# A blockwise triangular inverse on TensorE: transposed products of levels 1 and 2 moved from two array tiles to four

## The chip, the cores and the metric

One core of one Trainium2 chip. The metric is the device time of one execution in microseconds (us). The kernel before takes 3888.85 us (median of 3 runs, 3885.25 to 3891.66).

## The reference

Two transformer blocks of two layers each, on 512 tokens of width 1024, all in float32. The change touches only the first block's `rwkv7_bidir`, a linear recurrence over the tokens with 8 heads of 64, run forward and backward:

```python
def step(state, inp):
    r_t, w_t, k_t, v_t, kk_t, a_t = inp
    sa = jnp.einsum('bhij,bhj->bhi', state, -kk_t)
    state = (state * w_t[:, :, None, :] + sa[..., None] * (kk_t * a_t)[:, :, None, :]
             + v_t[..., None] * k_t[:, :, None, :])
    return state, jnp.einsum('bhij,bhj->bhi', state, r_t)
...
y = direction(0, False) + direction(1, True)
```

Everything else (pooling, differential attention, gates, feed-forward layers, the second block) is as before in both kernels.

## The kernel before, in words

The recurrence is done in chunks of 64 tokens. Within a chunk it needs the inverse of a unit triangular 64x64 matrix. There are 8 chunks, 8 heads and 2 directions: 128 such matrices in each of the two layers. They are worked on in 8 **groups** g of 16: g // 2 is the pair of heads, g % 2 the direction. A group's 16 matrices are numbered by q (0 to 3), e (which head) and p_ (which chunk of two). A half of the 128 partitions (`side(0)` or `side(1)`) holds one of two matrices.

The inverse is built by doubling. After a start X0, each **level** n (0 to 4, block sizes 2 to 32) does three products for each of the 16 matrices:

- `inv_a`: T1 = L X, which VectorE copies out of PSUM with a mask (line 1891, "the mask" below),
- `inv_x`: X' = X T1, copied out by ScalarE (line 1507),
- `inv_t`: the transpose of X', from T1 and XT, copied out by ScalarE (line 1507).

`inv_x` is left out at level 4. One product is a 64x64 by 64x64 matmul. It is float32, so it leaves two records in the trace: one step of 16 matmuls is 32 records, on PE (the matmuls) and on PEld (the weight loads). A 64x64 matmul uses one of four **array tiles**: the half of the array's rows is the half of the partitions that the operands stand on, the half of the columns is the half of the partitions of PSUM that the result goes to. A step uses all four tiles when the results of e = 1 cross to the other half, and two when none or all cross. In the kernel before the crossing is `p_ ^ e`:

| step | rows side | result side | tiles |
|---|---|---|---|
| `x0`, `r0`, `inv_a` 0, `inv_x` 0 | p_ | p_ | 2 |
| `inv_a` 1 to 4 | p_ | p_ ^ e | 4 |
| `inv_x` 1 to 3 | p_ ^ e | p_ | 4 |
| `inv_t` 0 | p_ | p_ ^ e | 4 |
| `inv_t` 1, 2, 3 | p_ ^ e | p_ ^ e | 2 |
| `inv_t` 4 | p_ ^ e | p_ | 4 |

A four-tile step writes to 256 columns of each of two neighbouring banks (`across`), a two-tile step to one bank.

**What sets the order.** Each engine runs its program in the order of one list of steps, made by `beats_of`: a group's beats are laid out one after the other, and group g + 1 starts 12 beats after group g. So while group g goes through its levels, TensorE also does the state chain of group g - 1 (`link` 1 to 7, some 8 matmuls each, whose state ScalarE copies), and VectorE and ScalarE do the preparation of group g + 1:

- `prep_w` on VectorE, after the mask of level 1: lines 1834 and 1835, and then 1837 where g + 1 is even, but 1840 and 1841 where g + 1 is odd (one instruction more),
- `prep_a`: four Exp on ScalarE, which wait for `prep_w`'s end, between the copies of level 1 and those of level 2; lines 1845 to 1850 on VectorE after the mask of level 2,
- `prep_b`, `prep_ar` on VectorE after the mask of level 3 (lines 1858 to 1868), which `gram` of g + 1 on TensorE waits for.

TensorE's order in one level is `inv_a` n, `link`, `inv_x` n, `inv_t` n, `link`, `inv_a` n + 1. `inv_a` n + 1 waits for ScalarE's copy of `inv_x` n; `inv_x` n waits for the mask of level n and the copy of `inv_t` n - 1. Each copy waits its turn behind what ScalarE has before it. `prep` of the last group's successor does not exist, so group 7 has no such neighbour, and group 0 has no `link` beside it. After group 7 the layer goes on with weights whose ring memory the recurrence had borrowed (`ring_back`).

## Time and profile before

| what | value |
|---|---|
| runs | 3885.25, 3891.66, 3888.85 us |
| the profiled execution | 3887.13 us, its span 3885.3 us |
| mean granted TensorE clock | 0.991 of full |
| PE busy | 3717.4 us (96%) |
| DVE, ACT, POOL busy | 43%, 37%, 36% |
| line 1891, the mask, in the first layer's recurrence | 32 x 0.69 us |

How to read it: PE is TensorE's matmuls, PEld its weight loads, DVE VectorE, ACT ScalarE, POOL GpSimd. The two recurrences lie at 98 to 375 us and 1216 to 1490 us of the span. Line 1134 is the helper that issues every matmul of the first block that is not a weight product, and line 1507 the one that issues every ScalarE instruction there, so a step is told by its place, its operands and its count: `inv_a` reads `arena,ring`, `inv_x` and `inv_t` read `arena` alone and follow each other in one row (x64). Group and level are written as (g, n).

### The profile page before, as it was taken

Reading aid. Unit: us, or ns where it says so; the run is one execution under the profiler, and the core shown is the slowest. Engines: PE = TensorE matmul, PEld = TensorE weight load, DVE = VectorE, ACT = ScalarE, POOL = GpSimd, SP = SyncE. Lnnn points to the kernel's source line nnn. Section 1 sums busy time; section 2 is a strip of 40 time slices with the busy share of each in tenths; the row PEclk is TensorE's granted clock in tenths of the full one; section 3 lists DMA queues with packets and bytes.
Section 4 is the critical chain, followed back from the end, with each engine's and each line's share of the span. In section 5 each row is a group of like instructions: output and inputs, shape, how many; then the busy total and the mean of one; then the engine's idle time right before and its main releaser. Section 6 shows DMA issues by size and latency. Waiting matters only on the chain.

```text
span 3885.3 us, 67218 instructions
## 1 busy us (share of the span) xinstructions
PE 3717.4 (96%) x28976; PEld 2990.7 (77%) x28976; DVE 1684.8 (43%) x2722; ACT 1448.4 (37%) x2468; POOL 1382.3 (36%) x581
## 2 busy tenths in 40 slices
PE   8888999999999898999999999999999999999999
PEld 7777768888887786687888876578888776688887
DVE  6554541477135554612683158515111377332112
ACT  3454252323324443522223243634222436433222
POOL 5001324444443002144444444234444353234443
PEclk9999999999999999999999999999999999999999
DMA  3001212266221001122473222112222221122222
GB/s 146 3 4 46 84 64 100 87 245 238 87 87 44 4 4 67 70 111 87 160 266 148 87 93 82 44 66 103 102 94 87 107 89 50 60 87 87 87 108 87
DMA packets 37151, 356.66 MB, mean 92 GB/s; under 512 B 4224, under 2 KB 4352, under 8 KB 17920
## 3 DMA queue, kind: packets, MB, share of 16 engines
q1 hardware_dynamic: 19584, 278.93, 19.4%
q10 hardware_dynamic: 17280, 73.48, 5.4%
q8 instruction: 232, 3.80, 0.4%
q14 instruction: 55, 0.45, 0.0%
HBM read 350.29 MB, written 2.10 MB: 91 GB/s over the span
## 4 chain that ended last, share of the span: by engine, by line
PE 84%; DVE 7%; ACT 4%; issue 2%; DMA 1%; PEld 1%; POOL 0%; PEldq 0%; DVEq 0%; SPq 0%; ACTq 0%; POOLq 0%
PE banks L768 23%; PE banks L770 23%; PE banks L769 23%; PE banks L1134 10%; PE banks L2200 3%; ACT arena L2356 2%; ACT arena L1507 2%; DMA ring<-stream 1%; PE banks L2282 1%; DVE arena L1996 1%; PE banks L1261 1%; DVE arena L1891 1%; DVE x L2757 0%; PE banks L1459 0%; DVE arena L2007 0%
## 5 line engine op out<-in xcount | busy, mean ns | idle before, releaser
L866 POOL TENSOR_TENSOR ring_r<-ring,hi_ring 128x1024 fp32r<-128x1024 f32 x490 | 1200.8, 2455 | 2174.0 <-ACT hi_ring L857 2173.4
L768 PE MATMUL banks<-xT_r,ring_r 128*128 128x512 f32 (+1 forms) x2480 | 949.0, 383 | 10.8 <-issue 6.8
L770 PE MATMUL banks<-xT_r,hi_ring 128*128 128x512 f32 x2096 | 826.5, 394 | 0.0
L769 PE MATMUL banks<-x_lo_r,hi_ring 128*128 128x512 f32 x2096 | 823.6, 393 | 0.0
L857 ACT ACTIVATE hi_ring<-ring 128x1024 fp32r<-128x1024 f32 x490 | 511.2, 1046 | 724.1 <-DMA ring<-stream 293.5
L768 PEld LDWEIGHTS banks<-xT_r,ring_r 128*128 128x128 f32 x2480 | 470.6, 190 | 105.2 <-issue 11.9
L770 PEld LDWEIGHTS banks<-xT_r,hi_ring 128*128 128x128 f32 x2096 | 394.5, 188 | 93.1
L769 PEld LDWEIGHTS banks<-x_lo_r,hi_ring 128*128 128x128 f32 x2096 | 396.3, 189 | 88.0 <-issue 1.4
L1134 PE MATMUL banks<-arena 64*64 64x64 f32 (+4 forms) x7456 | 342.4, 249 | 52.0 <-DVE arena L1891 22.8
L1507 ACT ACTIVATE arena<-banks 128x512 f32<-128x512 f32 x366 | 214.6, 596 | 388.6 <-PE banks L770 231.4
L770 PE MATMUL banks<-hi_ring,pairs 128*128 128x512 f32 x864 | 342.3, 396 | 0.0
L769 PE MATMUL banks<-ring_r,pairs 128*128 128x512 f32 x864 | 342.0, 396 | 0.0
L768 PE MATMUL banks<-hi_ring,pairs 128*128 128x512 f32 x864 | 340.6, 394 | 0.0
L1134 PEld LDWEIGHTS banks<-arena 64*64 64x64 f32 (+2 forms) x7456 | 262.4, 139 | 96.1 <-DVE arena L1891 27.8
L871 DVE TENSOR_TENSOR pairs<-arena,pairs 128x512 fp32r<-128x512 f32 x108 | 82.6, 765 | 430.8 <-ACT pairs L862 430.6
L2356 ACT ACTIVATE arena<-banks 128x512 f32<-128x512 f32 (+3 forms) x288 | 141.6, 504 | 306.2 <-PE banks L770 219.1
L1507 ACT ACTIVATE arena<-banks,small 128x512 f32<-128x512 f32 (+2 forms) x254 | 119.5, 482 | 255.8 <-PE banks L770 160.6
L769 PEld LDWEIGHTS banks<-ring_r,pairs 128*128 128x128 f32 x864 | 162.3, 188 | 39.7
L768 PEld LDWEIGHTS banks<-hi_ring,pairs 128*128 128x128 f32 x864 | 162.4, 188 | 39.3 <-POOL ring_r L866 0.8
L770 PEld LDWEIGHTS banks<-hi_ring,pairs 128*128 128x128 f32 x864 | 163.1, 189 | 37.0
L862 ACT ACTIVATE pairs<-arena 128x512 fp32r<-128x512 f32 x108 | 68.1, 631 | 311.9 <-PE banks L770 307.1
L769 PE MATMUL banks<-ring_r,xT_r 128*128 128x512 f32 (+1 forms) x448 | 169.9, 379 | 0.0
(274 smaller groups left out, 5400.3 us busy)
## 6 DMA issues: line engine op xcount, KB each, us to landing
ring<-stream SPq DMA_DIRECT2D x132, 2048.0 KB, 7.7
arena<-ada ACTq DMA_DIRECT2D x96, 512.0 KB, 4.9
arena<-ln_rows ACTq DMA_DIRECT2D x5, 1024.0 KB, 7.6
arena<-edge ACTq DMA_DIRECT2D x4, 1024.0 KB, 5.1
arena<-edge ACTq DMA_DIRECT2D x2, 1792.0 KB, 8.1
arena<-pack ACTq DMA_DIRECT2D x2, 1485.0 KB, 6.7
arena<-pack ACTq DMA_DIRECT2D x2, 1200.5 KB, 5.8
x<-x_in SPq DMA_DIRECT2D x4, 512.0 KB, 7.5
```

Of the source, the lines that this page charges most:

```text
L768: first = nc.tensor.matmul(out_, left[1], right[0], start=start, stop=False)
L769: low = nc.tensor.matmul(out_, left[0], right[1], start=False, stop=False)
L770: return first, low, nc.tensor.matmul(out_, left[0], right[0], start=False, stop=stop)
L857: nc.scalar.activation(feed.hi(n), feed.raw(n), ACT.Copy).then_inc(split_hi, 1)
L862: nc.scalar.activation(feed.hid_pair(n)[0], feed.hid[:, n, :], ACT.Copy).then_inc(hid_hi, 1)
L866: nc.gpsimd.tensor_tensor(feed.raw(n, ring_r), feed.raw(n), feed.hi(n).bitcast(F32), ALU.subtract).then_inc(split_lo, 1)
L871: nc.vector.tensor_tensor(lo, feed.hid[:, n, :], hi.bitcast(F32), ALU.subtract).then_inc(hid_lo, 1)
L1134: return nc.tensor.matmul(out_, lhsT, rhs, start=start, stop=stop)
L1261: ins = nc.tensor.transpose(bank[b][:, q * P:(q + 1) * P], src, C("ident"))
L1507: return nc.scalar.activation(out_, in_, func, **kw)
L2200: return nc.tensor.matmul(out_, lhsT, rhs, start=start, stop=stop)
L2356: return nc.scalar.activation(out_, in_, func, **kw)
```

## The change

The side that holds T1 and XT now depends on the level. `turned_side` gives it: p_ at levels 0 and 5, e at level 2, p_ ^ e at levels 1, 3 and 4. T1 of level n stands on the side of level n, and XT moves from the side of level n to the side of level n + 1 through `inv_t` n. So `inv_t` 1 goes from p_ ^ e to e and `inv_t` 2 from e to p_ ^ e: four tiles each. `inv_t` 3 stays at p_ ^ e, with two.

Four-tile products go to two banks. Bank 6 has no free neighbour, so `inv_t` 1 and 2 are written to the banks of the other direction (`2 - b0` and the next), which group g + 1 uses for `prep` before and for `gram` after. `inv_t` 1 therefore waits for `prep` of g + 1 to be copied out of both.

In all four-tile steps, those that had four tiles before too, the bank is now chosen by the array's rows side (it was e), and the four matmuls of one q are issued in the order of (result side, rows side): before, e was the outer loop and p_ the inner one. The copies follow the new places; `wu` reads XT at `p_ ^ e` instead of e. The number of matmuls and copies is the same.

```diff
-        banks_a, banks_x, banks_t = (b0,), (b0,) if n else (6,), (b0,) if n == 0 or last else (6,)
+        banks_a, banks_x, banks_t = (b0,), (b0,) if n else (6,), ((b0,), (2 - b0,), (2 - b0,), (6,), (b0,))[n]
...
-        return name == "inv_t" and level in (0, len(LEVELS) - 1) or name in ("inv_a", "inv_x") and level > 0
+        return name == "inv_t" and level != len(LEVELS) - 2 or name in ("inv_a", "inv_x") and level > 0
+
+    def turned_side(level, p_, e):
+
+        return p_ if level in (0, len(LEVELS)) else e if level == 2 else p_ ^ e
...
+                    if (name, args[1]) == ("inv_t", 1) and g < GROUPS - 1:
+                        drained(pe, uses, "prep", g + 1, only=1)
...
+                def turned_at(p_, e):
+                    return side(turned_side(level, p_, e)), turned_side(level - 1, p_, e) if 0 < level < len(LEVELS) - 1 else e
+
+                def tiles_of_array(p_, e):
+                    f = turned_side(level, p_, e)
+                    return (f, p_) if name == "inv_a" else (p_, f) if name == "inv_x" else (turned_side(level + 1, p_, e), f)
+
                 for q in range(4):
...
+                    for p_, e in sorted(HALVES, key=lambda pair: tiles_of_array(*pair)) if wide(name, level) else ():
+                        to, r = tiles_of_array(p_, e)
+                        h, i = turned_at(p_, e)
...
+                        ins = mm(across(banks[0])[side(to), r, q * CH:(q + 1) * CH], left, right, True, True)
...
-                            ins = mm(bank[banks[q // 2]][h, (q % 2 * 2 + e) * P:(q % 2 * 2 + e + 1) * P], XT[d][h, 2 * q + e, :],
+                            ins = mm(bank[banks[q // 2]][h, (q % 2 * 2 + e) * P:(q % 2 * 2 + e + 1) * P], XT[d][h, 2 * q + (p_ ^ e), :],
```

On TensorE, the first layer's group 1 at level 2: `inv_x` (rows 617 and 618), then `inv_t` (rows 619 and 620). Before:

```order
611 L1134 MATMUL banks<-arena 64x64 [waits halves_done,bank5_free]
612 L1134 MATMUL banks<-arena 64x64
613 L1134 MATMUL banks<-arena,ring 64x64 [waits bank5_free]
614 L1134 MATMUL banks<-arena,ring 64x64
615 L1134 MATMUL banks<-ring 64x64 x2
616 L1134 MATMUL banks<-arena 64x64 x2
617 L1134 MATMUL banks<-arena 64x64 [waits bank6_free,bank2_free]
618 L1134 MATMUL banks<-arena 64x64 x15
619 L1134 MATMUL banks<-arena 64x64 [waits bank6_free,bank2_free]
620 L1134 MATMUL banks<-arena 64x64 x15
```

(rows 611 to 616 are a `link` of group 0). The same place after:

```order
611 L1138 MATMUL banks<-arena 64x64 [waits halves_done,bank5_free]
612 L1138 MATMUL banks<-arena 64x64
613 L1138 MATMUL banks<-arena,ring 64x64 [waits bank5_free]
614 L1138 MATMUL banks<-arena,ring 64x64
615 L1138 MATMUL banks<-ring 64x64 x2
616 L1138 MATMUL banks<-arena 64x64 x2
617 L1138 MATMUL banks<-arena 64x64 [waits bank0_free,bank2_free]
618 L1138 MATMUL banks<-arena 64x64 x15
619 L1138 MATMUL banks<-arena 64x64 [waits bank0_free,bank2_free]
620 L1138 MATMUL banks<-arena 64x64 x15
```

Nothing moves: the steps stand in the same places, and the wait for bank 6 became one for bank 0.

On ScalarE, the copies of `inv_x` and `inv_t` of the same group at level 1 (rows 160, 161) and level 2 (rows 167, 168), as they stand after the change:

```order
160 L1525 ACTIVATE arena<-banks 128x2x4x64 [waits bank2_full]
161 L1525 ACTIVATE arena<-banks 128x2x4x64 [waits bank0_full]
162 L1525 ACTIVATE arena<-banks,small 128x64 [waits bank5_full]
163 L1525 ACTIVATE small<-arena 128x8 [waits prep_sum]
164 L1525 ACTIVATE arena<-arena 128x512 x2
165 L1525 ACTIVATE arena<-arena 128x512 [waits act_step]
166 L1525 ACTIVATE arena<-banks,small 128x64 [waits bank4_full]
167 L1525 ACTIVATE arena<-banks 128x2x4x64 [waits bank2_full]
168 L1525 ACTIVATE arena<-banks 128x2x4x64 [waits bank0_full]
```

Before, rows 161 and 168 were `arena<-banks 128x512 [waits bank6_full]`; the other rows and the order are the same. Rows 163 to 165 are `prep_a` of group 2: they stand ahead of the state copy (166) and of the copies of level 2.

## Rows read from the trace of the kernel before

**Rows 1.** The page, the chain that ended last, share of the span by line.

```profile
PE banks L768 23%; PE banks L770 23%; PE banks L769 23%; PE banks L1134 10%; PE banks L2200 3%; ACT arena L2356 2%; ACT arena L1507 2%; DMA ring<-stream 1%; PE banks L2282 1%; DVE arena L1996 1%; PE banks L1261 1%; DVE arena L1891 1%; DVE x L2757 0%; PE banks L1459 0%; DVE arena L2007 0%
```

**Rows 2.** Busy time by window, first recurrence: length, busy by engine (records), clock, DMA.

```profile
98.00:375.00 277.00, 241.53 (x6760) 209.50 (x6758) 139.09 (x215) 126.05 (x255) 0.93 (x1) 0.97 0.05 16
```

**Rows 3.** Timeline, weight loads, group 4: start, length, operation, count, [idle <-releaser].

```profile
247.11 1.07 PEld L1134 LDWEIGHTS banks<-arena,ring 64*64 64x64 f32 x30
...
253.49 1.51 PEld L1134 LDWEIGHTS banks<-arena 64*64 64x64 f32 x64 [0.52 <-DVE arena L1891]
...
255.33 0.60 PEld L1134 LDWEIGHTS banks<-arena,ring 64*64 64x64 f32 x30
...
257.14 1.96 PEld L1134 LDWEIGHTS banks<-arena 64*64 64x64 f32 x67 [0.56 <-DVE arena L1891]
```

**Rows 4.** Timeline, VectorE, group 4.

```profile
255.78 0.69 DVE L1841 TENSOR_TENSOR arena<-arena 128x512 f32<-128x512 f32 x1
256.39 0.68 DVE L1891 TENSOR_TENSOR arena<-banks,const 128x512 f32<-128x512 f32 x1
...
260.26 0.69 DVE L1891 TENSOR_TENSOR arena<-banks,const 128x512 f32<-128x512 f32 x1 [0.81 <-PE banks L1134]
```

**Rows 5.** Timeline, ScalarE, group 4.

```profile
256.62 1.79 ACT L1507 ACTIVATE arena<-arena 128x512 f32<-128x512 f32 x3
258.33 0.30 ACT L1507 ACTIVATE arena<-banks,small 128x64 f32<-128x64 f32 x1
258.52 1.07 ACT L1507 ACTIVATE arena<-banks 128x512 f32<-128x512 f32 x2
```

**Rows 6.** Timeline, weight loads, group 3.

```profile
226.07 0.60 PEld L1134 LDWEIGHTS banks<-arena,ring 64*64 64x64 f32 x32
...
229.67 0.60 PEld L1134 LDWEIGHTS banks<-arena,ring 64*64 64x64 f32 x32
...
233.71 1.08 PEld L1134 LDWEIGHTS banks<-arena 64*64 64x64 f32 x36 [0.45 <-DVE arena L1868]
```

**Rows 7.** Timeline, VectorE, group 3.

```profile
223.50 0.69 DVE L1891 TENSOR_TENSOR arena<-banks,const 128x512 f32<-128x512 f32 x1 [3.68 <-PE banks L1134]
...
225.82 0.69 DVE L1837 TENSOR_TENSOR arena<-arena 128x512 f32<-128x512 f32 x1
226.89 0.69 DVE L1891 TENSOR_TENSOR arena<-banks,const 128x512 f32<-128x512 f32 x1 [0.38 <-PE banks L1134]
```

**Rows 8.** Timeline, ScalarE, group 3.

```profile
225.05 0.60 ACT L1507 ACTIVATE arena<-banks 128x512 f32<-128x512 f32 x1 [1.15 <-PE banks L1134]
...
228.69 0.60 ACT L1507 ACTIVATE arena<-banks 128x512 f32<-128x512 f32 x1
```

**Rows 9.** Chain of waits, second layer, group 5: start, length, what.

```profile
1399.79 0.70 DVE arena L1891
...
1403.97 2.58 PE banks L1134 x108
```

**Rows 10.** Timeline, weight loads, group 7.

```profile
341.08 0.37 PEld L1134 LDWEIGHTS banks<-arena,ring 64*64 64x64 f32 x14
342.03 0.36 PEld L1134 LDWEIGHTS banks<-arena,ring 64*64 64x64 f32 x17 [0.58 <-issue]
```

**Rows 11.** Timeline, ScalarE, group 7.

```profile
340.06 0.60 ACT L1507 ACTIVATE arena<-banks 128x512 f32<-128x512 f32 x1 [1.15 <-PE banks L1134]
```

**Rows 12.** Busy time by window, first layer, group 0, around its level 2.

```profile
137.00:144.00 7.00, 5.71 (x151) 5.36 (x147) 5.10 (x9) 4.01 (x8) 0.00 (x0) 0.53 0.01 2
```

**Rows 13.** Timeline, ScalarE, group 0.

```profile
141.09 0.60 ACT L1507 ACTIVATE arena<-banks 128x512 f32<-128x512 f32 x1 [0.21 <-PE banks L1134]
```

**Rows 14.** Timeline, weight loads, group 0.

```profile
142.31 0.18 PEld L1134 LDWEIGHTS banks<-arena,ring 64*64 64x64 f32 x1
```

**Rows 15.** Timeline, weight loads: gram of group 3, then wu of group 2.

```profile
204.25 1.08 PEld L1134 LDWEIGHTS banks<-arena 64*64 64x64 f32 x36 [0.88 <-DVE arena L1868]
...
210.63 1.75 PEld L1134 LDWEIGHTS banks<-arena 64*64 64x64 f32 x32 [0.40 <-ACT arena L1507]
```

More of the change, by code:

```diff
@@ L1281, in step @@
                 level = args[1] if len(args) > 1 else 0
-                for q in range(4):
-                    for e in range(2):
-                        for p_ in range(2):
-                            n, straight, crossed = 2 * q + e, side(p_), side(p_ ^ e)
-                            h = crossed if level and name in ("inv_x", "inv_t") else straight
-                            to = crossed if name == "inv_a" and level or name == "inv_t" and level < len(LEVELS) - 1 else straight
-                            left, right = {"x0": (XT[d][h, n, :], C("ident2")[h]), "r0": (GM[d][h, q, e, 1, 0, :], V[g // 2 % 2][h, q, e, :]),
-                                           "inv_a": (GM[d][h, q, e, 0, 0, :], X[d][h, n, :]), "inv_x": (XT[d][h, n, :], T1[d][h, n, :]),
-                                           "inv_t": (T1[d][h, n, :], XT[d][h, n, :])}[name]
-                            at = (4 * e + q if wide(name, level) else n) * CH
-                            to = across(banks[0])[to, at:at + CH] if wide(name, level) else bank[banks[0]][to, at:at + CH]
-                            ins = mm(to, left, right, True, True)
+                def turned_at(p_, e):
+                    return side(turned_side(level, p_, e)), turned_side(level - 1, p_, e) if 0 < level < len(LEVELS) - 1 else e
@@ new lines, in tiles_of_array @@
+                def tiles_of_array(p_, e):
+                    f = turned_side(level, p_, e)
+                    return (f, p_) if name == "inv_a" else (p_, f) if name == "inv_x" else (turned_side(level + 1, p_, e), f)
+                for q in range(4):
+                    for p_, e in sorted(HALVES, key=lambda pair: tiles_of_array(*pair)) if wide(name, level) else ():
+                        to, r = tiles_of_array(p_, e)
+                        h, i = turned_at(p_, e)
+                        if name == "inv_a":
+                            i = turned_side(level - 1, p_, e) if level > 1 else e
+                            left, right = GM[d][side(p_), q, e, 0, 0, :], X[d][side(p_), 2 * q + i, :]
+                        else:
+                            left, right = XT[d][h, 2 * q + i, :], T1[d][h, 2 * q + (p_ if level else e), :]
+                            left, right = (left, right) if name == "inv_x" else (right, left)
+                        ins = mm(across(banks[0])[side(to), r, q * CH:(q + 1) * CH], left, right, True, True)
+                    for e, p_ in () if wide(name, level) else HALVES:
+                        h, n = turned_at(p_, e)[0] if name == "inv_t" else side(p_), 2 * q + e
+                        left, right = {"x0": (XT[d][h, n, :], C("ident2")[h]), "r0": (GM[d][h, q, e, 1, 0, :], V[g // 2 % 2][h, q, e, :]),
+                                       "inv_a": (GM[d][h, q, e, 0, 0, :], X[d][h, n, :]), "inv_x": (XT[d][h, n, :], T1[d][h, n, :]),
+                                       "inv_t": (T1[d][h, 2 * q + p_, :], XT[d][h, 2 * q + turned_at(p_, e)[1], :])}[name]
+                        ins = mm(bank[banks[0]][h, n * CH:(n + 1) * CH], left, right, True, True)
@@ L1581, in step @@
                 filled(b, n)
-                f((XT if name == "inv_t" else X)[args[0] % 2].rearrange("p (q e) t -> p e q t", e=2),
-                  across(b).rearrange("p (e q t) -> p e q t", e=2, q=4), ACT.Copy).then_inc(bank_free[b], 1)
+                f((XT if name == "inv_t" else X)[args[0] % 2].rearrange("p (q r) t -> p r q t", r=2),
+                  across(b).rearrange("p r (q t) -> p r q t", q=4), ACT.Copy).then_inc(bank_free[b], 1)
             elif name in ("x0", "inv_x", "inv_t"):
@@ L1890, in step @@
                 if wide(name, lev):
[L1891 to L1892 removed]
+                    V.tensor_tensor(T1[g % 2].rearrange("p (q r) t -> p r q t", r=2),
+                                    across(b).rearrange("p r (q t) -> p r q t", q=4),
+                                    masks.rearrange("p (r q) t -> p r q t", r=2), ALU.mult).then_inc(bank_free[b], 1)
                 else:
```

4 lines of the change are left out of this document (1 added, 3 removed).

## The prediction

> **What bounds the kernel now.** I read the chain by line first: three quarters of the span are the weight products of lines 768 to 770 and their kind, and line 1134, which holds the recurrence's small products, has 10% [rows 1]. So the change can only act inside the two recurrences. The window of the first shows PE busy for 241.5 of 277 us, VectorE for 139 and ScalarE for 126 [rows 2]; the second is nearly the same length (1216 to 1490 us). A busy share of 87% does not say that TensorE is the bound in each beat, because VectorE and ScalarE stand in the same loop. So I went to the timelines, engine by engine, and asked at each level what `inv_a` and `inv_x` wait for.
>
> **What the change takes off TensorE.** A two-tile step and a four-tile step of the same kind stand in one view: 30 loads of `inv_a` (4, 0) on two tiles take 1.07 us, 30 loads of `inv_a` (4, 2) on four take 0.60 us [rows 3]. The difference, 0.47 us, is what `inv_t` gives up at one level. The row of 1.51 us with 64 loads is `inv_x` (four tiles) and `inv_t` (two) one behind the other; it should become some 1.05 us. There are 2 levels x 8 groups x 2 layers = 32 such steps: 32 x 0.47 = 15.0 us of TensorE's time. That is the most that the change can bring, if each beat ended with TensorE.
>
> The Trainium skill speaks against this much (TensorE: Matmul & The Clock Gate, "Wait — 56ns, not 53.3ns?"): from one matmul's start to the next it never sees less than about 25 ns. By that a step of 32 records could not go under 0.80 us, and a new four-tile step would save some 0.15 us instead of 0.47 (an estimate from that page); every gain below would be a third, some 1.3 us in all. The 30 loads in 0.60 us [rows 3] are 20 ns apart at most, so this trace does not obey that floor and I give it no chance.
>
> **Even groups (2, 4, 6 in both layers, 0 in the second: seven).** Nothing, and this is the step that most of the forecast hangs on.
> Level 1: `inv_t` (4, 1) would end 0.47 earlier, and so could `link` and `inv_a` (4, 2), up to the point where the copy of `inv_x` is done. But the mask of level 2 starts at 256.39 with no idle time ahead of it, directly behind line 1841 of `prep_w` [rows 4]. VectorE's own queue from the mask of level 1 on sets that moment, however early `inv_a` (4, 2) comes. `inv_x` (4, 2) starts at 257.14 as before.
> Level 2: ScalarE does the Exps of `prep_a` from 256.62 to 258.41, then the state copy, and then the copy of `inv_x` at 258.52 with that of `inv_t` directly behind it [rows 5]. `inv_x` had been finished before (it is the first third of the row from 257.14 [rows 3]). `inv_a` (4, 3) waits for that copy, not for `inv_t`. The Exps wait for line 1841, which the change does not reach. So the mask of level 3 at 260.26, though it shows "0.81 <-PE" [rows 4], is late through ScalarE's queue, and `gram` of group 5 behind it keeps its time.
>
> **Odd groups with a successor (1, 3, 5 in both layers: six).** Here `prep_w` is one instruction shorter. In group 3 it ends at 226.51, and the mask of level 2 waits for PE until 226.89 [rows 7]. The copy of `inv_x` (3, 1) ends at 225.65 [rows 8], so `inv_a` (3, 2) can start some 0.06 later, at 225.71, instead of 226.07 [rows 6]: 0.36 earlier, and the mask too. At level 2 the copy of `inv_x` again stands behind the Exps and ends at 229.29 [rows 8], whatever TensorE does: `inv_a` (3, 3) starts at 229.35 instead of 229.67 [rows 6], and mask, `prep_b` and `gram` at 233.71 follow it. So group 3 gains 0.32, not 0.94. From the mask of level 1 (223.50) to that earliest start are 5.85 us. I hold it against a group without a disturbance, group 5 of the second layer: its mask of level 1 is at 1399.79 and `inv_a` (5, 3) ends at 1403.97 + 2.58 = 1406.55 [rows 9]. With 5.85 and the 0.74 that `inv_a` lasts it could end at 1406.38: 0.17. I take 0.25 for each of the six, between the two: 1.5 us.
>
> **Group 7 (twice).** No preparation runs beside it. The copy of `inv_x` (7, 1) ends at 340.66 [rows 11], `inv_a` (7, 2) started at 341.08 [rows 10] and can start at 340.72: 0.36. Level 2 has the same pattern. 2 levels x 2 layers x 0.36 = 1.4 us, all on the path, since the rest of the layer waits for group 7.
>
> **Group 0 of the first layer.** Here the mean granted clock is 0.53 [rows 12], so nearly all of this stretch runs at the lower level, 1.2 GHz, and a two-tile step is longer. The copy of `inv_x` (0, 2) ends at 141.69 [rows 13], so `inv_a` (0, 3) can start at 141.75 instead of 142.31 [rows 14]: 0.56. Level 1 can add between nothing and 0.47; I take 0.3. Together 0.9 us.
>
> **What costs.** One wait is added, in 14 places: `inv_t` 1 waits until `prep` of the next group has been copied out. Behind it in TensorE's queue stand a `link` and `inv_a`. `prep` is some 4 us older than `inv_t` 1 and its copies stand ahead of those of level 0, which `inv_a` 1 has already waited for, so I count nothing. `gram` of the next group now needs the banks of `inv_t` 2, whose copy `inv_x` 3 has waited for: nothing. ScalarE's copies of `inv_t` read two banks instead of one; the copies of `inv_x` do that now in the same 0.60 us [rows 8].
> The order and the banks of all other four-tile steps change too (7 steps of `inv_a` and `inv_x` and 2 of `inv_t` in each group, 144 in all). Their new pattern is that of `gram`: bank by rows side, (result, rows) in order. `gram` with four tiles and 128 columns takes 1.08 us for 36 loads (32 and a `link`'s 4), `wu` on two tiles and 128 columns 1.75 for 32 [rows 15]. So that pattern runs on four tiles. For 64 columns it is not in the trace: the bounds are no change and the two-tile rate, 0.47 more per step. I take no change.
>
> **The sum.** 1.5 + 1.4 + 0.9 = 3.8 us off the profiled execution: 3887.1 - 3.8 = 3883.3 us. That execution was 1.7 us under the median of the three runs, so for a median I say **3885.0 us**. A measurement of this kernel can tell about 0.2%, 7.8 us, from no change; its three runs alone spread over 6.4 us. My forecast is below that.
>
> **The rivals.**
> *TensorE was the bound after all* (12%). If what looks like cover moves along (the Exps of `prep_a` and the masks shift with the copies), the full 15.0 us come off: 3874. For it speaks PE's busy share in the window [rows 2]; against it, VectorE without idle time ahead of the mask [rows 4]. With half of it, 7.5 us, the time is 3881.
> *Instructions come too late* (9%, slower). TensorE stands still now and then in the middle of a step for want of instructions: 0.58 us inside `inv_a` (7, 2), put down to "issue" [rows 10]. Place: `inv_x`, `inv_t`, `link`, `inv_a` of levels 1 and 2, which now all run at the four-tile rate, 1.9 us in a row instead of 2.3. Price: some 0.6 to 0.8 us per new stop. If each of the 16 groups had one more on its path, 16 x 0.7 = 11.2 less the 3.8 gained is 7.4 slower: 3896. It decides from about 5 new stops for a gain lost, from 17 for a measurable loss. Against it: the same instructions are fetched, and in even groups a stop falls into the slack that the change widens. The Trainium skill (Runtime: NRT & Kernel Launch, "Instruction fetch mechanics") has instructions fetched in blocks ahead and calls this hidden by a slow issue; by it this rival would cost nothing. The row with 0.58 disagrees.
> *The new order halves the old four-tile steps* (4%, slower). Two matmuls with the same result side follow each other now. If they no longer ran side by side, 112 steps of `inv_a` and `inv_x` would cost 0.47 more, 53 us; with half of it covered 26, less 3.8: 3911. Rows 15 speak against it.
> *The change does nothing at all* to the time, since covers are wider than I read (15%): 3887 to 3889.
>
> **Chances.** My forecast has 60%, its own range 3881 to 3888. Faster by over 0.2%: the first rival and the edge of the forecast, 17%. Slower by over 0.2%: half of the second rival and the third with a share for a clock that falls in more places, 11%. Within 0.2%: 72%. The range 3877 to 3892 leaves out most of the first rival and the slow ends.
>
> **What would show it.** In the profile after: the x64 row of `inv_x` and `inv_t` at levels 1 and 2 near 1.05 us; the mask of level 2 in even groups still directly behind line 1841, and `inv_a` 3 still behind ScalarE's copy; in odd groups and group 7 `inv_a` 2 starting 0.06 us after the copy of `inv_x`; from the mask of level 1 to `gram` of the next group unchanged in even groups and 0.2 to 0.3 shorter in odd ones; line 1134's "issue" time as before. I am wrong if even groups become shorter, if `inv_a` alone takes over 0.7 us for its 32 loads, or if more than a handful of new "issue" stops stand in the levels.

## The result and the profile after: slower by 0.17%

| | median | runs | ratio to before, 95% |
|---|---|---|---|
| before | 3891.66 us | 19, 3883.51 to 3897.32 | 1 |
| changed | 3897.67 us | 19, 3892.70 to 3903.81 | 1.0017 [1.0011, 1.0023] |

0.17% of 3890 is 6.6 us slower; 3.8 us faster had been forecast. The profiled execution took 3895.01 us with a span of 3893.2, against 3887.13 and 3885.3. In these two executions the mean granted clock is the same 0.991. Over many executions it is not: the 19 of the changed kernel have 0.9891 on average, and the 114 of the kernel before that were timed beside the experiments have 0.9908 to 0.9911 in their four series. (The 19 of before in the table above have no clock on record.) What that is worth stands below, under "The clock as a rival".

What the change was to do to the array, it did. The view by windows has, in the columns of [rows 2], both recurrences of the changed kernel:

```profile
98.00:375.00 277.00, 234.34 (x6745) 201.06 (x6743) 137.92 (x212) 122.73 (x251) 0.00 (x0) 0.97 0.03 10
1216.00:1490.00 274.00, 234.09 (x6741) 200.88 (x6740) 137.42 (x212) 122.21 (x250) 2.41 (x1) 0.98 0.02 5
```

PE is busy for 7.2 us less than in [rows 2] in the first recurrence (and for 5.0 us less in the second, 239.06 before). It is idle longer, and the view of waits (engine, line, waited for: us in total, times, longest) says what the weight loads of the recurrence waited for. Before, first and second recurrence:

```profile
PEld banks L1134 <- issue: 18.6, 41, 1.3
...
PEld banks L1134 <- issue: 17.9, 41, 1.3
```

The changed kernel (its line 1138 is line 1134 of before, 1525 is 1507, 1909 is 1891):

```profile
PEld banks L1138 <- issue: 26.1, 50, 2.1
...
PEld banks L1138 <- issue: 24.1, 51, 1.6
```

"issue" is time in which TensorE waited for no engine and no transfer that the profile shows. It is 36.5 us before and 50.2 after (the two rows added), and a part of it is on the path. The chain of waits by line, first and second recurrence, before:

```profile
by line: PE banks L1134 58.1%; ACT arena L1507 10.2%; issue 6.1%; DVE arena L1891 3.7%; PE banks L1261 3.7%; PE banks L768 2.2%; PE banks L770 2.0%; PE banks L769 2.0%; DVE arena L1858 1.7%; DVE arena L1868 1.5%; DVE arena L1859 1.5%; DVE a
...
by line: PE banks L1134 55.7%; ACT arena L1507 11.1%; issue 5.3%; PE banks L1261 3.7%; DVE arena L1891 3.5%; PE banks L768 2.3%; PE banks L770 2.2%; PE banks L769 2.2%; DVE arena L1835 1.8%; DVE arena L1858 1.7%; DVE arena L1868 1.6%; DVE a
```

and changed:

```profile
by line: PE banks L1138 52.4%; ACT arena L1525 12.2%; issue 7.8%; PE banks L1265 3.6%; DVE arena L1909 3.0%; DMA ring<-stream 2.8%; PE banks L768 2.2%; PE banks L770 2.0%; PE banks L769 2.0%; DVE arena L1853 1.8%; DVE arena L1876 1.2%; DVE 
...
by line: PE banks L1138 52.9%; ACT arena L1525 11.7%; issue 7.0%; PE banks L1265 3.4%; DVE arena L1909 3.3%; PE banks L768 2.6%; PE banks L770 2.5%; PE banks L769 2.4%; DVE arena L1853 1.8%; DVE arena L1876 1.7%; DVE arena L1886 1.6%; DVE a
```

The share of "issue" rises by 1.7% of the window in both: 1.7% x (277 + 274) = 9.4 us more on the path. This is a sign and no sum, since other shares move by as much: PE's line falls by 5.7% and 2.8%, ScalarE's rises by 2.0% and 0.6%, and a transfer of 2.8% stands in the first chain of the changed kernel.

**Where the time goes.** The masks are the same instructions in both kernels, four in each group, so the time from one to the next can be compared place by place. From the first group's mask of level 1 to group 7's last, the first recurrence takes 216.90 us before (135.19 to 352.09) and 219.62 changed (136.01 to 355.64), the second 213.79 (1254.57 to 1468.37) and 217.67 (1256.37 to 1474.04). That is 6.6 us more, of the 7.9 us between the two profiled spans. All 62 intervals, changed less before, in us:

| groups | mask 1 to 2 | mask 2 to 3 | mask 3 to 4 | to the next group's first |
|---|---|---|---|---|
| group 0 of the first layer | -0.3 | -0.7 | +0.7 | 0.0 |
| odd, with a successor (six) | -1.5 | +3.4 | 0.0 | +1.0 |
| even (seven) | +0.2 | +3.5 | +0.1 | -0.2 |
| group 7 (twice) | -0.5 | +0.7 | +0.1 | |

So there is a gain from level 1 to level 2, in the odd groups and in group 7, and it is more than lost from level 2 to level 3, in even groups as well. The largest single losses are group 2's in both layers, 1.5 us each. VectorE's masks of levels 1, 2 and 3 there, first layer, before and changed, and the weight load of the changed kernel that makes the third one late:

```profile
193.73 0.69 DVE L1891 TENSOR_TENSOR arena<-banks,const 128x512 f32<-128x512 f32 x1 [3.68 <-PE banks L1134]
197.38 0.68 DVE L1891 TENSOR_TENSOR arena<-banks,const 128x512 f32<-128x512 f32 x1
201.11 0.69 DVE L1891 TENSOR_TENSOR arena<-banks,const 128x512 f32<-128x512 f32 x1 [0.67 <-PE banks L1134]
```
```profile
195.00 0.69 DVE L1909 TENSOR_TENSOR arena<-banks,const 128x512 f32<-128x512 f32 x1 [3.68 <-PE banks L1138]
198.65 0.68 DVE L1909 TENSOR_TENSOR arena<-banks,const 128x512 f32<-128x512 f32 x1
203.88 0.69 DVE L1909 TENSOR_TENSOR arena<-banks,const 128x512 f32<-128x512 f32 x1 [2.17 <-PE banks L1138]
```
```profile
203.21 0.37 PEld L1138 LDWEIGHTS banks<-arena,ring 64*64 64x64 f32 x18 [1.38 <-issue]
```

The last row is the second part of `inv_a` (2, 3): TensorE stood for 1.38 us in the middle of the step.

**Where a stop lies.** Group 7 of the first layer, weight loads, changed kernel (it answers to [rows 10]):

```profile
342.87 1.12 PEld L1138 LDWEIGHTS banks<-arena 64*64 64x64 f32 x67 [0.50 <-DVE arena L1909]
...
344.37 0.30 PEld L1138 LDWEIGHTS banks<-arena,ring 64*64 64x64 f32 x11
345.09 0.37 PEld L1138 LDWEIGHTS banks<-arena,ring 64*64 64x64 f32 x19 [0.42 <-issue]
...
347.97 0.24 PEld L1138 LDWEIGHTS banks<-arena,ring 64*64 64x64 f32 x8
350.34 0.44 PEld L1138 LDWEIGHTS banks<-arena,ring 64*64 64x64 f32 x24 [2.14 <-issue]
...
355.24 1.25 PEld L1138 LDWEIGHTS banks<-arena,ring 64*64 64x64 f32 x38 [1.43 <-issue]
```

`inv_a` (7, 2) stops for 0.42 us, `inv_a` (7, 3) for 2.14, each in the middle of a step. From stop to stop, here and behind the stop of group 2 above, the windows show (length, PE, PEld, DVE, ACT, POOL, clock, DMA share, GB/s):

```profile
345.09:350.34 5.25, 2.88 (x126) 2.60 (x125) 0.69 (x1) 1.60 (x4) 0.00 (x0) 1.00 0.01 3
203.21:208.35 5.14, 3.62 (x126) 3.24 (x126) 3.26 (x6) 1.51 (x3) 0.00 (x0) 1.00 0.02 3
```

Some 126 matmuls, as many loads and a few semaphore instructions: 256 TensorE instructions. Counted through the whole trace, every stop of over 0.3 us inside a step lies at the same remainder of the instruction's number by 256. The page names the carrier:

```profile
q8 instruction: 232, 3.80, 0.4%
```

232 packets of 16384 bytes (3.80 MB) for TensorE's 59540 instructions: 256 in a packet, 64 bytes each. A packet takes 0.9 to 1.5 us. Of the changed kernel's 101 blocks in the two recurrences, 30 begin with such a stop, and in 29 of these the first instruction comes 1.2 to 1.6 us after the packet's end. So these stops are waits for a block of instructions. I call the place where one block ends and the next begins a **border**. Stops of over 0.3 us at borders: 13 with 10.2 us before, 30 with 26.1 us in the changed kernel.

That also shows why the recurrence is sensitive. A level is three steps of 64 instructions (32 loads, 32 matmuls), two `link`s of 32 and 5 semaphore instructions: 261, about one block. It lasts 3.60 us in group 3 of the kernel before (`inv_a` at 226.07 and 229.67 [rows 6]).

### The profile page after: what moved, and what is told of

It reads as the page before. It is cut to its first block, busy times and chain, and to the rows that moved or that the text cites. A ratio compares the mean times of both kernels' runs of the same rounds, so it can differ in the third digit from the quotient of the medians.

```text
span 3893.2 us, 67232 instructions
## 1 busy us (share of the span) xinstructions
PE 3709.0 (95%) x28976; PEld 2978.1 (76%) x28976; DVE 1695.7 (44%) x2722; ACT 1446.9 (37%) x2468; POOL 1384.3 (36%) x581
## 4 chain that ended last, share of the span: by engine, by line
PE 82%; DVE 8%; ACT 4%; issue 3%; DMA 1%; POOL 1%; PEld 1%; PEldq 0%; DVEq 0%; ACTq 0%; SPq 0%; POOLq 0%
PE banks L768 23%; PE banks L770 22%; PE banks L769 22%; PE banks L1138 9%; PE banks L2219 3%; ACT arena L1525 2%; ACT arena L2375 2%; PE banks L2301 1%; DMA ring<-stream 1%; DVE arena L2015 1%; DVE arena L2701 1%; PE banks L1265 0%; DVE arena L2700 0%; DVE x L2776 0%; DVE arena L1909 0%
## 5 line engine op out<-in xcount | busy, mean ns | idle before, releaser
L1138 PE MATMUL banks<-arena 64*64 64x64 f32 (+4 forms) x7456 | 333.3, 251 | 58.8 <-DVE arena L1909 25.8
L1138 PEld LDWEIGHTS banks<-arena 64*64 64x64 f32 (+2 forms) x7456 | 252.0, 140 | 101.9 <-issue 31.5
L768 PEld LDWEIGHTS banks<-hi_ring,pairs 128*128 128x128 f32 x864 | 162.4, 188 | 39.4 <-POOL ring_r L866 0.8
```

Source lines behind the costliest of these rows:

```text
L768: first = nc.tensor.matmul(out_, left[1], right[0], start=start, stop=False)
L1138: return nc.tensor.matmul(out_, lhsT, rhs, start=start, stop=stop)
```

## The experiments

In all of them "time" is a median, with its ratio to the kernel before, timed beside it, and the 95% interval. The medians of before in these series go from 3888.68 to 3891.66 us, so the ratios are to be compared and not the times. "Issue" is the sum of the two rows of the view of waits (36.5 us before, 50.2 changed). "Stops" are those of over 0.3 us at borders.

**1. The order and the banks alone, and one level alone.** The order and the banks of all other four-tile steps as in the changed kernel, but `inv_t` 1 and 2 on two tiles in bank 6, and without the added wait for `prep`:

```diff
-        banks_t = ((b0,), (2 - b0,), (2 - b0,), (6,), (b0,))[n]
+        banks_t = ((b0,), (6,), (6,), (6,), (b0,))[n]
-        return name == "inv_t" and level != len(LEVELS) - 2 or ...
+        return name == "inv_t" and level in (0, len(LEVELS) - 1) or ...
-        return p_ if level in (0, len(LEVELS)) else e if level == 2 else p_ ^ e
+        return p_ if level in (0, len(LEVELS)) else p_ ^ e
...
-                    if (name, args[1]) == ("inv_t", 1) and g < GROUPS - 1:
+                    if (name, args[1]) == ("inv_t", -1) and g < GROUPS - 1:
```

> The changed kernel with the side of T1 and XT at p_ ^ e on all levels 1 to 4, so inv_t 1 and 2 have two array tiles and bank 6 again. Kept of the change: in all four-tile steps the bank is chosen by rows side and the four matmuls of a q are issued in the new order. Theory A (instructions come too late: with four tiles in inv_t 1 and 2 the levels use up a block of 256 TensorE instructions faster than the next one arrives, 29 stops for want of instructions in both recurrences instead of 13): the time is that of before, within 2 us, with about 13 stops of together some 10 us. Theory B (the new order or banks cost time in the old four-tile steps): all of the loss is here, some 6 to 7 us above before. Theory C (the waits for the other direction's banks): as before.

Then four tiles at level 1 only (`level in (0, 1, ...)`, banks `(2 - b0,)` there), and at level 2 only; the wait for `prep` stands at the `inv_t` that has four tiles. In these two, two products of a two-tile `inv_t` go to the same place, so a part of XT is lost; the instructions and their tiles are those named.

> Four tiles in inv_t at level 1 alone; level 2 keeps two tiles and bank 6. Theory A: stops lie between 13 and 29 and the time between before and the changed kernel, 0 to 6 us above before; not simply half, since where a block ends is a matter of place. Theory B: the full 6 to 7 us. Theory C (the wait of inv_t 1 for prep of the next group, which is here): the full loss here, none with level 2 alone.

> Four tiles in inv_t at level 2 alone; level 1 keeps two tiles and bank 6. Theory A: as with level 1 alone, 0 to 6 us above before and 13 to 29 stops. Theory B: the full 6 to 7 us. Theory C: no loss, since level 2 comes 4 us after the wait for prep's copies matters.

| run | time | ratio | issue | stops |
|---|---|---|---|---|
| order and banks alone | 3888.57 us | 0.9995 [0.9986, 1.0004] | 32.7 us | 12, 8.6 us |
| level 1 alone | 3893.86 us | 1.0013 [1.0004, 1.0022] | 44.2 us | 27, 20.6 us |
| level 2 alone | 3892.64 us | 0.9998 [0.9989, 1.0007] | 38.9 us | 19, 13.7 us |

The order and the banks cost nothing that an interval of 0.1% (3.5 us) can tell, and the 26 to 53 us of the prediction's rival are ruled out. The loss comes back with four tiles at level 1. With level 2 alone there is none, though "issue" and stops grow there too. Taken by themselves, these two rows are also what the theory of the added wait had forecast, the full loss at level 1 and none at level 2; experiment 3 has to decide on that. The recurrences' own lengths, taken from mask to mask as above, are 427.8 us for the order alone, 434.8 for level 1, 428.6 for level 2, with 430.7 before and 437.3 changed.

**2. How fast can TensorE get instructions?** The kernel before, with 256 extra products on four tiles (512 weight loads and 512 matmuls, four blocks) and then 256 on two, before the first `gram`, without a wait between them (the wait for the two banks is moved ahead of them):

```diff
+                if (layer, g, n) == (0, 0, 0):
+                    c0 = CONST["gram0"][0]
+                    for tiles in (4, 2):
+                        for turn in range(64 if tiles == 4 else 64):
+                            for to, r in sorted(HALVES) if tiles == 4 else ((0, 0), (1, 1), (0, 0), (1, 1)):
+                                mm(bank[banks[r]][side(to), turn % 8 * CH:(turn % 8 + 1) * CH], const[side(r), c0:c0 + CH],
+                                   const[side(r), c0 + CH:c0 + 2 * CH], True, True)
```

> The kernel before, and ahead of the first gram of the first layer 256 products of 64x64 by 64x64 of constants on four tiles, in the changed order and banks, and then 256 on two tiles; no wait inside, results overwritten by gram. Each half is 1024 TensorE instructions (512 weight loads, 512 matmuls), four blocks of 256. By the array alone the first half takes 512 x 14.4 ns = 7.4 us and the second 512 x 29 ns = 14.8 us. Theory A: the supply sets both; stops every 256 instructions, 3.5 to 5.2 us from one to the next, 14 to 20 us for each half. If the supply were not a bound (rivals B, C): 7.4 and 14.8 us and no stops. B would show in a first half without stops but longer than 7.4 us.

It took 3917.68 us in its one execution. Timeline of the weight loads (start, length, operation, count, idle before):

```profile
124.61 1.96 PEld L1134 LDWEIGHTS banks<-const 64*64 64x64 f32 x128 [1.08 <-issue]
128.06 1.95 PEld L1134 LDWEIGHTS banks<-const 64*64 64x64 f32 x128 [1.50 <-issue]
131.52 2.82 PEld L1134 LDWEIGHTS banks<-const 64*64 64x64 f32 x128 [1.50 <-issue]
135.52 3.81 PEld L1134 LDWEIGHTS banks<-const 64*64 64x64 f32 x128 [1.18 <-issue]
139.52 3.81 PEld L1134 LDWEIGHTS banks<-const 64*64 64x64 f32 x128 [0.20 <-issue]
```

This is the clearest measurement of the study. The array does 128 loads and their matmuls on four tiles in 1.96 us, but the next 128 begin 3.45 us after the first: 1.50 us of standing still at each of the two borders behind a block that is all on four tiles. The row of 131.52 holds the change from four tiles to two: 2.82 us, then 1.18 us of standing still. On two tiles alone the same number takes 3.81 us and the stop is 0.20. Four tiles are worth 1.85 us of array time per block, of which 0.55 arrive (4.00 to 3.45 us). At 3.45 us a block an instruction costs 13.5 ns, though the array does one in 7.7 ns here (1.96 us for 256). The first half as a whole was a miss: it took 11.9 us (120.65 to 132.52), where 14 to 20 were expected; at its start TensorE still had part of a block at hand, and the borders behind it lie 3.45 us apart, the low end of the 3.5 to 5.2 expected. The second half took 16.9 us.

**3. The added wait alone.** As the first run of experiment 1, but with the changed kernel's wait for `prep` (14 places):

```diff
-                    if (name, args[1]) == ("inv_t", -1) and g < GROUPS - 1:
+                    if (name, args[1]) == ("inv_t", 1) and g < GROUPS - 1:
```

> The changed kernel with the transposed products of levels 1 and 2 on two tiles and in bank 6, as in the run of the order alone, but with the changed kernel's wait for the next group's preparation at inv_t of level 1 (14 places). Theory C (that wait or what it orders costs the time): 3894 to 3898 us, as the changed kernel. Theory A: no instruction comes faster than before and few are added, so stops of 9 to 11 us in sum and the time within 1.5 us of the run of the order alone: a ratio of 0.9990 to 1.0004 against before.

3891.91 us, 1.0001 [0.9992, 1.0010]; issue 39.0 us, stops 20 with 14.2 us, where 9 to 11 us of stops were expected. The ratio is in the range of the supply theory, the median 3.3 us above the run without the wait where 1.5 were allowed. The 14 waits are 14 instructions more, so the borders drift too, and the two can't be told apart here. Without four tiles in `inv_t` 1 and 2 the wait brings no loss to the kernel before that its interval (0.1%) can tell, which answers the question that experiment 1 left. Not tested is the wait together with four tiles, so that what it costs there is open.

**4. Moving the borders.** Waits on a semaphore long set, put where TensorE waits anyway; two of them are one instruction, each 0.106 us. They are to change nothing behind them but where the borders fall. In the kernels with 16, 32 and 64 instructions they stand ahead of the first `gram`:

```diff
                 A, B = ARI[g % 3], BB[g % 2]
+                for _ in range(K if (layer, g) == (0, 0) else 0):
+                    pe.wait_ge(const_loaded, 16)
                 if n == 0:
```

The loop runs once for each half of the first `gram`, so it adds 2 K waits, which are K instructions (K = 16, 32 or 64). The first three expectations leave open whether waits or instructions count; the traces show 32 and 64 instructions. The added waits are not quite free: TensorE stands for 1.9 and 1.8 us at this place with 16 or 32 instructions more, for 1.9 and 3.1 with 64, so that the last cost 1.3 us. All of this is put down to "issue" and is contained in that column below, 3.6 us (4.9 at 64) in both kernels alike, but not in the rows 0 and "64, elsewhere".

> The same with half as many extra waits (32 ahead of each of the two parts), so that the blocks' borders lie a quarter of a block or less from those of the changed kernel. Theory A: stops of over 0.3 us again at the same remainder by 256 and at a third set of steps; number 25 to 35, sum 22 to 34 us; time 3894 to 3904 us. Theories B and C: stops at the steps of the changed kernel, time within 1 us of it.

> The changed kernel with 64 more waits on the constants' semaphore in TensorE's stream ahead of the first gram of group 0 and 64 ahead of its second part (a semaphore that has long been set, so that they wait for nothing), packed two to an instruction: if they all stand ahead of the recurrence, every later TensorE instruction is 64 or 128 places further on in the stream; TensorE is waiting for the preparation there anyway. Theory A (a block of 256 TensorE instructions comes too late; the stops lie where the stream passes from one block to the next): all stops of over 0.3 us in the recurrences still lie at the same remainder of the instruction's number by 256, so at other steps of the program than in the changed kernel: the stops of 1.5 us within inv_a of group 2, level 3 and of 2.3 us within inv_a of group 7, level 3 are gone from there. Their number stays near 30 and their sum within 22 to 34 us (26 in the changed kernel), the time within 3 us below to 6 us above the changed kernel's: 3894 to 3904 us. Theory C (a bank or the earlier wait for the next group's preparation) and theory B (the order of the products): the stops stay at the same steps, since the steps, banks and waits are the same, and the time within 1 us.

> The kernel before with the same extra waits as in the run with half as many. Theory A: the 13 stops of the kernel before lie at other steps; their sum 8 to 15 us (10 before), the time within 2 us below to 4 us above the kernel before: a ratio of 0.9995 to 1.001. Theories B and C: stops at the same steps and the same time.

Then the same 64 instructions in the kernel before, and 16 in both:

> The kernel before with the same extra waits as the changed kernel has in its run with 64 more instructions (the profiles of the last runs show how far these waits shift the stream: two waits are one instruction, so 32 and 64 instructions, an eighth and a quarter of a block, not 64 and 128). They cost 1.3 us at the first gram, as there. Theory A: stops of 8 to 15 us in sum, at other steps than in the kernel before; with the 1.3 us a time of 3889 to 3894 us. If the change's worth hangs on where the blocks' borders fall, the changed kernel at this place (3891.2 us) stands 3 us below to 3 us above this one, not 6.6 us above as without a shift. If the loss of the changed kernel had nothing to do with the borders, this run would be at 3884 to 3886 us.

> The changed kernel with 16 more instructions ahead of the recurrence, in TensorE's waits for the first group's preparation (8 in each). Theory A: stops of over 0.3 us 20 to 30, 16 to 26 us in sum, at the same remainder by 256; a time between those at a shift of 0 and of 32 instructions: 3890 to 3898 us. Without a part of the borders in it: 3897 to 3898 us, as the changed kernel.

> The kernel before with the same 16 instructions. Theory A: 8 to 15 us of stops, 3889 to 3892 us; the changed kernel at this shift is 0 to 7 us above it.

Last 96 in both, 64 of them in TensorE's first waits for the input, and 64 in the changed kernel all at that place:

```diff
                     pe.wait_ge(ident_loaded, 16)
+                for _ in range(64 if (layer, which) == (0, 2) and tt < 2 else 0):
+                    pe.wait_ge(ident_loaded, 16)
```

> The changed kernel with 96 more instructions ahead of the recurrence, as empty waits: 64 of them (32 and 32) in TensorE's first two waits for the input, some 12 and 4 us long, and 32 in its waits for the first group's preparation. They should cost nothing by themselves. The supply of instructions: 20 to 30 stops of 18 to 27 us, at steps again other than before; 3888 to 3898 us. If the loss depends on where the borders fall, this kernel stands 2 us below to 8 us above the kernel before at the same shift; if the runs at 0 and 16 were above it for another reason than the borders, it would stand 6 to 8 us above.

> The kernel before with the same 96 instructions. The supply of instructions: 8 to 14 us of stops, 3887 to 3892 us.

> The changed kernel at the shift of 64 instructions once more, but with the extra instructions in the waits for the input, so that the 1.3 us at the first gram should be saved. If the position of the borders sets the stops: stops over 1 us at the steps that had them in the other run with 64 (inv_x of group 1 at level 2, links of group 2, layer 1's inv_a of group 3 at level 3 and links of group 5), a sum of 19 to 26 us and 3889 to 3891 us. If the stops fall at random from run to run, they lie elsewhere in at least half of these places.

| shift | before: time, ratio | changed: time, ratio | changed less before | issue, before / changed | stops, before / changed |
|---|---|---|---|---|---|
| 0 | 3891.66, 1 | 3897.67, 1.0017 [1.0011, 1.0023] | +0.17% | 36.5 / 50.2 | 10.2 / 26.1 |
| 16 | 3888.39, 1.0002 [0.9993, 1.0011] | 3896.67, 1.0019 [1.0008, 1.0029] | +0.17% | 39.4 / 51.7 | 11.2 / 21.3 |
| 32 | 3889.86, 0.9998 [0.9989, 1.0007] | 3891.03, 1.0003 [0.9995, 1.0012] | +0.05% | 36.2 / 46.0 | 8.3 / 18.7 |
| 64 | 3891.54, 1.0003 [0.9994, 1.0012] | 3891.17, 1.0006 [0.9997, 1.0015] | +0.03% | 42.9 / 50.7 | 12.8 / 22.4 |
| 64, elsewhere | | 3889.84, 1.0001 [0.9992, 1.0010] | | 45.0 | 19.8 |
| 96 | 3891.61, 1.0010 [1.0001, 1.0019] | 3895.27, 1.0021 [1.0012, 1.0030] | +0.11% | 41.4 / 50.3 | 13.3 / 23.1 |

The stops did move as expected: with 32 or 64 instructions more, `inv_a` (2, 3) and `inv_a` (7, 3) of the first layer have none, and all stops are again at the same remainder. The times of the first two of these runs, 3891 us, were a miss: I had put them at 3894 to 3904, holding the place of the borders for a matter of 3 us. By the ratios (1.0017 to 1.0003) it is worth 5 to 6 us to the changed kernel, nearly the whole loss. The stops of the run with 32 were a miss too: 18.7 us, where 22 to 34 were expected. The kernel before at shift 16 took 3888.39 us, just under the 3889 to 3892 expected.

The last run put the borders of shift 64 there in another way. 25 of its 30 stops lie at the very instruction at which the first run with 64 had one. Three of the four places named came back at over 1 us, the fourth at 0.66. The `link` (2, 4) and layer 1's `inv_a` (3, 3), in the run with 64 at the first `gram` (weight loads):

```profile
229.13 0.13 PEld L1138 LDWEIGHTS banks<-arena 64*64 64x64 f32 x1 [1.66 <-issue]
...
1349.83 0.21 PEld L1138 LDWEIGHTS banks<-arena,ring 64*64 64x64 f32 x8 [1.65 <-issue]
```

and with 64 at the input:

```profile
225.34 0.13 PEld L1138 LDWEIGHTS banks<-arena 64*64 64x64 f32 x1 [1.93 <-issue]
...
1344.86 0.21 PEld L1138 LDWEIGHTS banks<-arena,ring 64*64 64x64 f32 x8 [1.67 <-issue]
```

So most stops are no chance of an execution; they belong to the program's layout. At none of five layouts is the changed kernel faster than its twin by the ratios; at 32 and 64 the two can't be told apart. The mean of the differences is +0.11%, 4 us. No kernel run beats the one before by more than its interval.

The lengths of the two recurrences together, mask to mask in the profiled executions, show the same order of size at the place itself, before / changed: 430.7 / 437.3 us at shift 0, 431.0 / 434.6 at 16, 428.8 / 431.8 at 32, 430.4 / 430.3 at 64 (430.0 elsewhere), 431.5 / 434.6 at 96. Each is one execution.

**The clock as a rival.** The changed kernel and its shifted forms have a lower mean granted clock, 0.9889 to 0.9898, than the kernel before and its shifted forms, 0.9898 to 0.9911. Time goes with it inside one kernel: of the 114 executions of before, the 16 at 0.989 take 3894.1 us on average, the 33 at 0.991 3890.3 and the 39 at 0.992 3887.2. A straight line of one slope through the executions of all kernels gives 2.0 us for each 0.001. The changed kernel's own executions, at the same granted clock, take 3898.4 us at 0.989 and 3895.3 at 0.991. So some 4 to 5 us of its loss stay at an equal clock and 2 to 4 us go with the lower one. An estimate with these 2.0 us taken out gives, changed less before, +4.3 us at shift 0, +2.5 at 16, -0.8 at 32, +0.9 at 64 and +2.3 at 96, each within about 2 us: a mean of 1.8 in place of 4. The place of the borders is still worth some 5 us to the changed kernel. In the profiled pair the granted clock of the recurrences' windows hardly differs, 0.97 and 0.99 before, 0.97 and 0.98 changed. Whether the change itself lowers the clock, or the stops do, no run isolates.

## Why the prediction was wrong, by its steps

**The array's share: right.** The x64 row of `inv_x` and `inv_t` was to be near 1.05 us. Group 4, weight loads, changed (it answers to [rows 3]):

```profile
256.12 1.06 PEld L1138 LDWEIGHTS banks<-arena 64*64 64x64 f32 x65 [0.52 <-DVE arena L1909]
```

**Even groups: the covers held, the "nothing" did not.** VectorE, group 4: the mask of level 2 at 259.01 is still directly behind the last line of `prep_w` (1859 is 1841 of before), without idle time ahead, as in [rows 4]. ScalarE's copy at 261.15 is still behind the Exps, as in [rows 5]. From mask 1 to mask 2 five of the seven even groups are within 0.01 us of before, and the other two 0.08 and 0.14 longer. But from mask 2 to mask 3 the seven lose 3.5 us, nearly all in group 2 (1.5 in each layer) and in group 0 of the second layer (0.5). The prediction had held that in even groups a stop falls into slack; the two largest losses are there.

```profile
258.40 0.69 DVE L1859 TENSOR_TENSOR arena<-arena 128x512 f32<-128x512 f32 x1
259.01 0.68 DVE L1909 TENSOR_TENSOR arena<-banks,const 128x512 f32<-128x512 f32 x1
```
```profile
259.25 1.80 ACT L1525 ACTIVATE arena<-arena 128x512 f32<-128x512 f32 x3
260.95 0.29 ACT L1525 ACTIVATE arena<-banks,small 128x64 f32<-128x64 f32 x1
261.15 1.28 ACT L1525 ACTIVATE arena<-banks 128x512 f32<-128x512 f32 x2
```

**Odd groups and group 7: the gain came, and was taken at the next border.** Group 3, VectorE and weight loads, changed:

```profile
225.97 0.69 DVE L1909 TENSOR_TENSOR arena<-banks,const 128x512 f32<-128x512 f32 x1 [3.68 <-PE banks L1138]
```
```profile
228.28 0.59 PEld L1138 LDWEIGHTS banks<-arena,ring 64*64 64x64 f32 x32
...
229.82 0.42 PEld L1138 LDWEIGHTS banks<-arena 64*64 64x64 f32 x18 [0.31 <-DVE arena L1909]
230.98 0.79 PEld L1138 LDWEIGHTS banks<-arena 64*64 64x64 f32 x48 [0.74 <-issue]
...
232.20 0.59 PEld L1138 LDWEIGHTS banks<-arena,ring 64*64 64x64 f32 x32
...
234.95 2.32 PEld L1138 LDWEIGHTS banks<-arena 64*64 64x64 f32 x76 [0.67 <-issue]
```

From the mask of level 1 to `inv_a` (3, 2) it is 2.31 us (228.28 - 225.97) where it was 2.57 (226.07 - 223.50 [rows 6, 7]): 0.26 gained, 0.36 foreseen. Over all six odd groups mask 2 comes 1.5 us sooner after mask 1, the very 1.5 of the prediction's term, and mask 3 3.4 us later after mask 2. Level 2 of group 3 shows how: the level is shorter than its block of instructions takes to come. `inv_x` (3, 2) stops for 0.74 us after 18 loads, and `inv_a` (3, 3) comes 3.92 us after `inv_a` (3, 2), not 3.60 as in [rows 6]. In group 7, `inv_a` (7, 2) starts at 344.37, straight behind the copy, as foreseen; the stops of 0.42 and 2.14 us shown above follow.

**Group 0 of the first layer: not told by these profiles.** From the mask of level 1 to `inv_a` (0, 3) it is 6.29 us (136.01 to 142.30) where it was 7.12 (135.19 to 142.31): 0.83 shorter, with 0.86 foreseen. But the granted clock of 137 to 144 us is 0.80 where it was 0.53 [rows 12], so the agreement may be the clock's.

**What was counted at nothing.** Order and banks were nothing that the interval can tell (experiment 1). Its copies of `inv_t` 1 and 2 read one bank, so the wide reads were not tested by themselves; in the changed kernel the two copies of a level take 1.08 us together at 231.49 and at 343.66, against 1.07 in [rows 5]. The added wait was nothing that the range of its run can tell (experiment 3). One estimate in the prediction is worked out wrongly: from the floor of 25 ns a four-tile step of 30 loads would take 0.75 us and save 0.32 against the 1.07 of [rows 3], not 0.15. Nothing else used it.

**The step that failed** is the last one of "what would show it": *line 1134's "issue" time as before*. It was the silent assumption of every term, that TensorE's instructions come as fast as the array can take them. I had the row that speaks against it, 0.58 us in the middle of `inv_a` (7, 2) [rows 10], and gave it 9% as the rival "instructions come too late". That rival named the place and the mechanism. Its time was 3896, on a median of before that later came out 2.8 us higher; the 7.4 us slower that it named came out as 6.6 by the ratio. That is in part luck, with 16 stops at 0.7 us on the path in its sum and 17 more at 0.9, not all of them on the path, in the traces. Two reasons held it down, and both were wrong:

- *The same instructions are fetched.* They are, but the rate is what counts. Experiment 2 puts a block of 256 instructions at 3.45 us, and the 261 of a level at 3.5. It is no sharp floor: the shortest blocks in the two kernels' recurrences took 3.3 us (263.57 to 266.88 us in the kernel before). A level lasted 3.60 us, so the kernel before stood 0.1 to 0.25 us from this bound, and the forecast took 0.25 to 0.36 us off such levels.
- *A price of 0.6 to 0.8 us per stop.* Stops of 1.5 to 2.2 us came. 17 more stops with 15.9 us more in sum are 0.9 each.

The Trainium skill (Runtime: NRT & Kernel Launch, "Instruction fetch mechanics") has TensorE's instructions come in blocks of 256 by a queue of their own, which this trace bears out with its 232 packets of 16384 bytes. It calls the crossing of a border mostly hidden, since instructions are issued more slowly than they are fetched. For 64x64 products on four tiles that doesn't hold here: 1.50 us at each border behind a full four-tile block of experiment 2.

**How much was given back.** Of the 15.0 us that were to leave the array's time by the prediction's count (the two windows show 12.2 us less of PE, with a few records fewer in them), 13.7 stand in the "issue" rows (50.2 - 36.5), at the shifts of 16, 32, 64 and 96 it is 12.3, 9.8, 7.8 and 8.9 us. The loss of time is largest at the two shifts where that is largest.

**What stays open.** The supply bound explains that nothing is gained, not that something is lost. A packet starts some 1.2 us after the border ahead of it where blocks follow fast, but 2.1 to 2.6 us after it ahead of most stops of over 1.4 us. It starts later than 1.8 us in 13 of the 101 blocks before and in 20 of the changed kernel. What delays it, no run here tells. How much of the loss is the late packets' and how much the lower clock's is open too. Nor did I isolate whether the 3.8 us of gain are earned in full at the shifts where the two kernels tie.

## What to carry to other kernels

Before making TensorE's small products faster, count its instructions per microsecond of the loop (loads, matmuls and waits; a float32 product is two of each). If 256 of them take near 3.5 us, expect array time that is taken off to come back as "issue". Fewer instructions should help there; no run here tried that. A few stops of "issue" in the middle of a step are the sign of it; a difference of 0.1 to 0.2% between two such kernels can be the layout of their blocks, so compare them at several shifts, and compare the mean granted clock of all executions, not of the profiled one alone.

## What the runs showed of the hardware

- Instruction supply of TensorE: one packet of 16384 bytes for 256 instructions; 0.9 to 1.5 us for the packet, 1.2 to 1.6 us from its end to the block's first instruction after a stop; 3.45 us from border to border in experiment 2, 3.3 at the shortest in the recurrences.
- 128 loads with their matmuls on four 64x64 tiles take 1.96 us, 15.3 ns each, on two tiles 3.81 us, 29.8 ns each.
- 16 to 96 instructions that do nothing, ahead of a loop, change the time of a kernel by up to 5 to 6 us (ratios 1.0017 and 1.0003 to the kernel before), with the borders at other instructions.
- An instruction of two waits on a semaphore that is already set takes TensorE 0.106 us.
- At a mean granted clock of 0.989 the kernel before takes 3894.1 us (16 executions), at 0.992 3887.2 (39).
